# Redealing the opening of a hybrid decoder layer: one load moved to ScalarE's queue, waits by bank, weight splits in another order, forget gates later and their series on VectorE

## The chip, the cores and the metric

The kernel runs on one core of a Trainium2 chip. The metric is the device time of one execution in microseconds. The kernel before was run three times; the profile is a fourth execution, taken by the hardware profiler. All times within it count from its first instruction.

## The reference, cut to what matters

One decoder layer over x of 512 x 2048, in float32:

```python
h = rms_norm(x, g_pre)
proj = einsum('bsd,de->bse', h, w_in)          # q, k, v, gate of three head groups, and six forget logits
out_a = moba_attention(...)                    # 6 heads, causal, T5 bias
log_f = log_sigmoid(fb + b_forget)
out_b = forgetting_attention(..., log_f)       # 6 heads, bias by the running sum of log_f
mkv = einsum('bmd,de->bme', rms_norm(mem, g_mem), w_mem_kv)
out_m = memory_attention(...)                  # 4 heads into 256 memory tokens
y = concatenate([out * silu(gate) for each group])
o = einsum('bse,ed->bsd', y, w_out)
x = x + rms_norm(o, g_post)
```

## The kernel before, in words

**Numbers.** Every large product runs at float32 precision as three passes: an operand is split into a high half (ScalarE copies it to the rounded type) and a low half (VectorE subtracts the high half), and `three` multiplies high x high, low x high, high x low. So each weight piece of 128 x 1024 goes: DMA into `raw`, ScalarE to `ring` half 0 (L985, `hi`), VectorE to `ring` half 1 (L1394, `minus`), TensorE. `ring` has three slots, so the high half of piece n waits until piece n-3 is used; `raw` has six.

**Stages.** First the memory part: 256 memory tokens are turned by TensorE (`turn_tiles(0, ...)`), taken from PSUM by ScalarE (`hi_memory`) and VectorE (`lo_memory`) in eight banks, and multiplied with w_mem_kv in eight strips of two pieces each (`strip`; `hi_mem`, `lo_mem`). Strips 0 to 3 give K, 4 to 7 give V; VectorE scales each by the token norms (`k_mem`, `copy_v_mem`), which TensorE spreads over the partitions by `spread_rstd` in strip 1. During strips 1 to 5 the x tiles are squared, scaled, turned in strips 3 to 6 and taken as tokens (`take_tokens`, L1053 to L1061 and L1479). The bias table of the T5 heads is made by TensorE in strip 3 and copied by VectorE (L1629) in strip 5.

Then 28 projection pairs of 128 columns each. Both dimensions are halved, and each pair takes seven products (TOK_A to TOK_G) of 128 x 1024 weights by 1024 x 256 tokens instead of eight; some operands are sums of weight quarters (VectorE, L1421, `add_weights`) or of token quarters. Four token operands are "late" (TOK_B, C, E, G): `hi_late` and `lo_late` split them after the last strip, in `LATE_ORDER`. The attention of the head before is dealt over the products of a pair (`attention`, `after_operand`). Pairs 0 to 3 are queries and gates of the memory heads; pair 4 on are the other heads.

The forget logits are six columns; `forget_gates` multiplies them as a narrow stationary operand `wf` with four token operands, TOK_E last, before pair 0. ScalarE and VectorE sum the two halves in `fbuf` (L1222, L1668), POOL makes -|z| (L1884, L1885, which raises f_neg), ScalarE takes Exp in pair 0 (L1236), VectorE a reciprocal at the end of pair 1 (L1690), and POOL the series of the logarithm (L1890 to L1898) on 6 x 512 values. VectorE scans the sum at the end of pair 3 (L1693).

Last the output projection, in the same way, in 52 steps of one piece each (`STEPS`; five ring slots). Each step is 12 matmuls of 128 x 512. `y_work(n)` deals the making of its token operands over the steps: VectorE makes TOK_B at n = 6, TOK_C's sum at 8, TOK_B's low half at 9.

**What sets the order.** Everything is written out by hand: each engine runs its own list in order and waits on semaphores. SyncE issues all loads of weights in the order of use; whatever it waits for holds up all loads behind it. It loads g_post (L603, L604) between steps 10 and 11, once `y_raw` has told that the last head is gated, because g_post lies where its gate buffer was. ScalarE issues only two loads at the very start (L1170).

What the steps of the change touch: in the tensor block L645 (`strip`), L814, L821, L849, L850; in the scalar block L1065, L1174 to L1222, L1234, L1346; in the vector block L1456, L1596 to L1669, L1688; in the gpsimd block L1889 to L1898; in the sync block L603, L604.

## Time and profile before

| | us |
|---|---|
| median of 3 runs | 918.08 |
| lowest, highest | 917.96, 918.86 |
| the profiled execution, its own time | 920.29 |
| its span, first to last instruction | 918.5 |
| busy TensorE (PE), VectorE (DVE), ScalarE (ACT), GpSimd (POOL) | 884.9, 694.8, 503.6, 106.1 |
| mean granted TensorE clock | 0.985 |

Matmuls are pipelined, so a busy TensorE says only that it has work; gaps and the granted clock say where it has lost time. A granted clock of 1.00 is 2.4 GHz, 0.50 is 1.2 GHz. In a row of the timeline the first number is the start, the second the length of the merged stretch, and the brackets give the idle time before it and what ended it.

### The profile page before, as it was taken

How to read it: one execution, taken by the hardware profiler on the slowest of the kernel's cores; microseconds unless marked ns; L12 is line 12 of the kernel's file. 1: busy time of each engine (PE TensorE's matmuls, PEld its weight loads, DVE VectorE, ACT ScalarE, POOL GpSimd, SP SyncE). 2: the span in 40 equal slices, each digit the busy share in tenths (PEclk: the TensorE clock that was granted, in tenths of full speed). 3: DMA queues.
4: the chain of work that ended last, by engine and by line, in shares of the span. 5: the costliest groups of instructions: out<-in, count | busy, mean ns of one | idle time of the engine just before them, and what ended most of it. 6: DMA issues, size and time to landing. Idle time of an engine off the chain costs nothing.

```text
span 918.5 us, 16262 instructions
## 1 busy us (share of the span) xinstructions
PE 884.9 (96%) x6525; PEld 841.8 (92%) x6525; DVE 694.8 (76%) x965; ACT 503.6 (55%) x882; POOL 106.1 (12%) x103
## 2 busy tenths in 40 slices
PE   8997998999999999999999999999999999799995
PEld 5887998999999999999999999999999988688884
DVE  4889978987777777777777778787877784975558
ACT  5795554555646464646464646464646474555552
POOL 0000406811111001010021212020202000000000
PEclk9999999999999999999999999999999999899998
DMA  9955476469979566975567774444444496466755
GB/s 299 294 135 151 145 246 194 112 128 201 195 145 197 129 195 133 265 151 142 167 155 160 230 166 111 104 103 105 104 104 104 159 359 225 151 209 198 282 198 184
DMA packets 178641, 161.54 MB, mean 176 GB/s; under 512 B 6969, under 2 KB 143833, under 8 KB 177286
## 3 DMA queue, kind: packets, MB, share of 16 engines
q1 hardware_dynamic: 169574, 142.67, 51.6%
q0 software_dynamic: 8704, 16.78, 12.5%
q8 instruction: 52, 0.85, 0.4%
q10 hardware_dynamic: 288, 1.05, 0.3%
q14 instruction: 23, 0.19, 0.1%
HBM read 152.33 MB, written 43.28 MB: 213 GB/s over the span
## 4 chain that ended last, share of the span: by engine, by line
PE 79%; DVE 13%; ACT 5%; issue 3%; DVEq 0%; POOL 0%; ACTq 0%; POOLq 0%
PE d_ps L630 12%; PE d_ps L632 12%; PE d_ps L631 12%; PE e_ps L630 6%; PE e_ps L632 6%; PE e_ps L631 6%; PE c_ps L630 3%; PE c_ps L632 3%; PE c_ps L631 3%; DVE ring L1394 3%; PE pt_ps L777 3%; PE score_ps L631 1%; PE score_ps L630 1%; PE score_ps L632 1%; DVE sums L1421 1%
## 5 line engine op out<-in xcount | busy, mean ns | idle before, releaser
L1394 DVE TENSOR_TENSOR ring<-raw,ring 128x1024 fp32r<-128x1024 f32 x134 | 165.2, 1237 | 67.9 <-ACT ring L985 67.4
L1394 DVE TENSOR_TENSOR ring<-sums,ring 128x1024 fp32r<-128x1024 f32 x112 | 140.2, 1253 | 96.1 <-ACT ring L985 95.7
L630 PE MATMUL d_ps<-tok_hi,ring 128*128 128x256 f32 x672 | 191.7, 285 | 2.9 <-DVE ring L1394 2.9
L632 PE MATMUL d_ps<-tok_lo,ring 128*128 128x256 f32 x672 | 190.8, 284 | 0.0
L631 PE MATMUL d_ps<-tok_hi,ring 128*128 128x256 f32 x672 | 190.7, 284 | 0.0
L985 ACT ACTIVATE ring<-raw 128x1024 fp32r<-128x1024 f32 x134 | 141.3, 1059 | 72.9 <-PE d_ps L632 46.8
L630 PEld LDWEIGHTS d_ps<-tok_hi,ring 128*128 128x128 f32 x672 | 129.5, 193 | 3.3 <-issue 3.3
L632 PEld LDWEIGHTS d_ps<-tok_lo,ring 128*128 128x128 f32 x672 | 129.6, 193 | 0.0
L631 PEld LDWEIGHTS d_ps<-tok_hi,ring 128*128 128x128 f32 x672 | 129.5, 193 | 0.0
L985 ACT ACTIVATE ring<-sums 128x1024 fp32r<-128x1024 f32 x112 | 117.9, 1053 | 19.8 <-DVE sums L1421 18.1
L1421 DVE TENSOR_TENSOR sums<-raw 128x1024 f32<-128x1024 f32 x56 | 70.2, 1253 | 0.6 <-issue 0.3
L1421 DVE TENSOR_TENSOR sums<-sums,raw 128x1024 f32<-128x1024 f32 x56 | 70.3, 1255 | 0.0
L630 PE MATMUL c_ps<-tok,ring 128*128 128x256 f32 x224 | 64.4, 287 | 0.0
L630 PE MATMUL e_ps<-tok_hi,ring 128*128 128x256 f32 x224 | 64.3, 287 | 0.0
L630 PE MATMUL e_ps<-tok,ring 128*128 128x256 f32 x224 | 64.3, 287 | 0.0
L632 PE MATMUL e_ps<-tok_lo,ring 128*128 128x256 f32 x224 | 63.4, 283 | 0.0
L631 PE MATMUL d_ps<-tok,ring 128*128 128x256 f32 x224 | 63.4, 283 | 0.0
L632 PE MATMUL d_ps<-tok,ring 128*128 128x256 f32 x224 | 63.4, 283 | 0.0
L632 PE MATMUL c_ps<-tok,ring 128*128 128x256 f32 x224 | 63.4, 283 | 0.0
L630 PE MATMUL d_ps<-tok,ring 128*128 128x256 f32 x224 | 63.4, 283 | 0.0
L631 PE MATMUL e_ps<-tok_hi,ring 128*128 128x256 f32 x224 | 63.4, 283 | 0.0
L631 PE MATMUL c_ps<-tok,ring 128*128 128x256 f32 x224 | 63.4, 283 | 0.0
(375 smaller groups left out, 2204.7 us busy)
## 6 DMA issues: line engine op xcount, KB each, us to landing
raw<-in_w_in_dram SPq DMA_DIRECT2D x112, 512.0 KB, 6.2
sum_dram<-in_w_out_dram POOLq DMA_DIRECT2D x32, 512.0 KB, 7.4
raw<-sum_dram SPq DMA_DIRECT2D x32, 512.0 KB, 3.8
raw<-in_w_out_dram SPq DMA_DIRECT2D x24, 512.0 KB, 6.4
raw<-in_w_mem_kv_dram SPq DMA_DIRECT2D x16, 512.0 KB, 8.3
sum_dram<-in_w_out_dram SPq DMA_DIRECT2D x4, 2048.0 KB, 11.9
stage<-in_x_dram SPq DMA_DIRECT2D x4, 1024.0 KB, 9.5
xres<-in_x_dram SPq DMA_DIRECT2D x4, 1024.0 KB, 7.3
```

What stands on the lines that cost most here:

```text
L630: pe.matmul(dst, lhs[0], rhs[0], start=start, stop=False, skip_group_check=True)
L631: pe.matmul(dst, lhs[1], rhs[0], start=False, stop=False, skip_group_check=True)
L632: return pe.matmul(dst, lhs[0], rhs[1], start=False, stop=stop, skip_group_check=True)
L777: last = pe.matmul(bank[:, first:S], v, pT[:, hl_p, kb, first:S] if not head.memory else pT_mem[:, hl_p, kb, first:S], start=(hl_v, hl_p, ...
L985: act.activation(dst, src, ACTF.Copy).then_inc(hi_done, 1)
L1394: return dve.tensor_tensor(dst, a_, hi_.bitcast(F32), ALU.subtract)
L1421: dve.tensor_tensor(sum_tile(p, s), one, two, ALU.add).then_inc(sum_done, 1)
```

## The change

The load of g_post leaves SyncE's list. ScalarE issues it in step 5 of the output projection, after its own wait for the same semaphore:

```diff
@@ sync
             load_steps(9, 11)
-            sp.wait_ge(y_raw, NH)
-            sp.dma_start(gpost[:], g_post.partition_broadcast(P)[:, 0, :]).then_inc(gpost_landed, 16)
             load_steps(11, X_AFTER[0])
@@ scalar, y_work
                 if n == 5:
                     act.wait_ge(y_raw, NH)
+                    act.dma_start(gpost[:], g_post.partition_broadcast(P)[:, 0, :]).then_inc(gpost_landed, 16)
                     hi_y(TOK_D, LAST_TILE, LAST_TILE + 1)
```

TensorE's two waits for four and eight banks of memory tokens become one wait per bank inside strip 0. The splits of weights and tokens are dealt in another order on ScalarE and VectorE: weight pieces go between the banks and ahead of other work of a strip, and the table copies go from VectorE to ScalarE.

```diff
@@ tensor
+                        if t == 0 and k % 2 == 0:
+                            pe.wait_ge(bank_taken, kt // 2 + 1)
                         last = three(d_ps[t % 2][:, 0:NMEM], (w[:, 0, k], w[:, 1, k]), (memT[:, 0, kt], memT[:, 1, kt]),
...
-                if t == 0:
-                    pe.wait_ge(bank_taken, 8)
...
-            pe.wait_ge(bank_taken, 4)
@@ scalar
             hi_memory(2, 4)
-            hi_memory(4, 6)
             hi_mem(1)
-            hi_memory(6, 8)
+            hi_memory(4, 8)
             for t in range(STRIPS_MEM):
...
-                hi_next(0)
+                if t != 1:
+                    hi_next(0)
+                hi_next(1)
                 if 1 <= t <= NM:
...
-                hi_next(1)
+                if t == NM + 1:
+                    for i, (bank, lo_, hi_) in enumerate(table_banks):
+                        act.wait_ge(table_made, i + 1)
+                        act.activation(table[:, lo_:hi_], bank[0:NA, 0:hi_ - lo_], ACTF.Copy).then_inc(table_copied, 1)
                 if t == 0:
...
                     root(1, 0, MB)
+                    hi_mem(4)
@@ vector
-            lo_memory(0)
+            lo_memory(0, 2)
             lo_mem(0)
+            lo_memory(2, 4)
             lo_mem(1)
-            lo_memory(1)
+            lo_memory(4, 8)
...
+            def lo_next(t, half):
+                if t + 1 < STRIPS_MEM:
+                    lo_mem(2 * (t + 1) + half)
+                else:
+                    add_weights(0, half + 1)
+                    lo_operand(0, half)
             for t in range(STRIPS_MEM):
+                if t > 0:
+                    lo_next(t, 0)
                 if t == 1:
...
+                if t > NM:
+                    copy_v_mem(t - 1)
+                if t == 0:
+                    lo_next(t, 0)
+                lo_next(t, 1)
                 if 1 <= t <= NM:
...
-                if t > NM:
-                    copy_v_mem(t - 1)
-                for half in range(2):
-                    if t + 1 < STRIPS_MEM:
-                        lo_mem(2 * (t + 1) + half)
-                    else:
-                        add_weights(0, half + 1)
-                        lo_operand(0, half)
-                if t == NM + 1:
-                    for i, (bank, lo_, hi_) in enumerate(table_banks):
-                        dve.wait_ge(table_made, i + 1)
-                        dve.tensor_copy(table[:, lo_:hi_], bank[0:NA, 0:hi_ - lo_]).then_inc(table_copied, 1)
```

The late operands come in the order B, C, E, G. The splits of E and G, and the gate products with TOK_E, move into pair 0, and so does what follows from them. `wf` lies at the place of `pT` and is cleared by POOL after 16 turned banks instead of by VectorE in strip 4.

```diff
-LATE_ORDER = [TOK_E, TOK_B, TOK_C, TOK_G]
+LATE_ORDER = [TOK_B, TOK_C, TOK_E, TOK_G]
@@ tensor
-            pe.wait_ge(late_ready, 1)
-            forget_gates(2, TOK_E, slice(T2, S), final=True).then_inc(f_done, 1)
...
                     product(p, i)
+                    if p == 0 and i == TOK_D:
+                        pe.wait_ge(late_ready, LATE_ORDER.index(TOK_E) + 1)
+                        forget_gates(2, TOK_E, slice(T2, S), final=True).then_inc(f_done, 1)
                     attention(p, i)
@@ scalar, after the strips
-            hi_late(TOK_E)
+            hi_late(TOK_B)
             hi_v_mem(2)
             hi_operand(0, 2)
-            hi_late(TOK_B)
             hi_v_mem(3)
             hi_late(TOK_C)
-            hi_late(TOK_G)
-            act.wait_ge(f_done, 1)
-            act.activation(fbuf[:, 1], f_ps[32:32 + NB, :], ACTF.Copy).then_inc(f_low, 1)
@@ scalar, after_operand
-                if p == 0 and i == TOK_D:
+                if p == 0 and i == TOK_A:
+                    hi_late(TOK_E)
+                if p == 0 and i == TOK_B:
+                    hi_late(TOK_G)
+                if p == 0 and i == TOK_E:
+                    act.wait_ge(f_done, 1)
+                    act.activation(fbuf[:, 1], f_ps[32:32 + NB, :], ACTF.Copy).then_inc(f_low, 1)
+                if p == 0 and i == TOK_G:
                     act.wait_ge(f_neg, 1)
                     act.activation(fbuf[:, 1], fbuf[:, 2], ACTF.Exp).then_inc(f_exp, 1)
@@ vector, after the strips
-            dve.tensor_tensor(token_f32(TOK_G), token_f32(TOK_G), token_f32(TOK_C), ALU.subtract).then_inc(late_f32, 1)
-            lo_late(TOK_E)
+            lo_late(TOK_B)
             lo_v_mem(2)
             lo_operand(0, 2)
-            lo_late(TOK_B)
+            dve.tensor_tensor(token_f32(TOK_G), token_f32(TOK_G), token_f32(TOK_C), ALU.subtract).then_inc(late_f32, 1)
             lo_v_mem(3)
             lo_late(TOK_C)
-            lo_late(TOK_G)
-            dve.wait_ge(f_low, 1)
-            dve.scalar_tensor_tensor(out=fbuf[:, 0], in0=f_ps[0:NB, :], scalar=bfor[:, 0:1], in1=fbuf[:, 1],
-                                     op0=ALU.add, op1=ALU.add).then_inc(f_z, 1)
@@ vector, after_operand
+                if p == 0 and i == TOK_B:
+                    lo_late(TOK_E)
+                if p == 0 and i == TOK_C:
+                    lo_late(TOK_G)
+                if p == 0 and i == TOK_E:
+                    dve.wait_ge(f_low, 1)
+                    dve.scalar_tensor_tensor(out=fbuf[:, 0], in0=f_ps[0:NB, :], scalar=bfor[:, 0:1], in1=fbuf[:, 1],
+                                             op0=ALU.add, op1=ALU.add).then_inc(f_z, 1)
@@ gpsimd
+            pool.wait_ge(bank_turned, 16)
+            pool.memset(wf[:].bitcast(F32), 0.0).then_inc(wf_cleared, 1)
```

The series leaves POOL, where it was 21 instructions, for VectorE, where multiply and add go together: 12 instructions, one after each product of pair 2 and the first five of pair 3, each waiting for the one before.

```diff
@@ vector
+            def forget_series(n):
+                z, e, s2, p = fbuf[:, 0], fbuf[:, 1], fbuf[:, 2], fbuf[:, 3]
+                last = len(SERIES) + 3
+                if n > last:
+                    return
+                dve.wait_ge(f_series, n + 1)
+                if n == 0:
+                    dve.tensor_tensor(e, e, p, ALU.mult).then_inc(f_series, 1)
+                elif n == 1:
+                    dve.tensor_tensor(s2, e, e, ALU.mult).then_inc(f_series, 1)
+                elif n == 2:
+                    dve.tensor_scalar(p, s2, SERIES[0], None, ALU.mult).then_inc(f_series, 1)
+                elif n < last - 1:
+                    dve.scalar_tensor_tensor(out=p, in0=p, scalar=SERIES[n - 2], in1=s2, op0=ALU.add, op1=ALU.mult
+                                             ).then_inc(f_series, 1)
...
+                if 2 <= p < NM:
+                    forget_series(PRODUCTS * (p - 2) + i)
@@ gpsimd
-            pool.wait_ge(f_rec, 1)
-            chain(pool.tensor_tensor(e, e, p, ALU.mult))
...
-            pool.tensor_tensor(z, p, z, ALU.subtract).then_inc(f_parts, 1)
```

## Rows read from the trace of the kernel before

**Rows 1.** The page, section 2: slices of the span, TensorE's granted clock.

```profile
PEclk9999999999999999999999999999999999899998
```

**Rows 2.** Waits of TensorE over the whole span: who for whom, us, times, longest.

```profile
PE c_ps L630 <- issue: 5.5, 1, 5.5
```

**Rows 3.** Windows by stage: opening, pairs 1 to 4, the restart at 786.73.

```profile
13.97:96.20 82.23, 69.50 (x528) 66.08 (x528) 74.78 (x144) 60.01 (x107) 0.00 (x0) 0.94 0.70 200
...
116.36:140.21 23.85, 23.85 (x196) 23.59 (x195) 17.70 (x26) 14.42 (x29) 0.00 (x0) 1.00 0.72 226
140.21:169.08 28.87, 26.04 (x196) 25.27 (x194) 25.33 (x28) 13.37 (x29) 22.76 (x14) 0.94 0.53 156
169.08:194.24 25.16, 24.35 (x196) 23.68 (x194) 21.57 (x27) 13.89 (x29) 12.49 (x9) 1.00 0.66 137
194.24:218.28 24.04, 24.04 (x196) 23.66 (x194) 19.76 (x29) 14.34 (x31) 2.96 (x4) 1.00 0.82 176
...
786.73:791.98 5.25, 5.25 (x12) 4.14 (x13) 5.25 (x5) 2.03 (x3) 0.00 (x0) 0.50 0.44 154
```

**Rows 4.** Timeline of SyncE before the output projection's step 11.

```profile
748.26 3.58 SPq L507 DMA_DIRECT2D raw<-in_w_out_dram  x2
765.59 0.34 SPq L604 DMA_DIRECT2D gpost<-in_g_post_dram  x1
```

**Rows 5.** Timeline of ScalarE in the output projection, steps 5 to 7.

```profile
764.97 1.06 ACT L985 ACTIVATE ring<-raw 128x1024 fp32r<-128x1024 f32 x1 [1.66 <-PE score_ps L632]
...
772.42 1.06 ACT L985 ACTIVATE ring<-raw 128x1024 fp32r<-128x1024 f32 x1 [6.08 <-DMA raw<-in_w_out_dram]
...
775.29 0.58 ACT L1307 ACTIVATE waste_o<-score_ps 128x512 bf16<-128x512 f32 x1
...
776.97 1.92 ACT L1276 ACTIVATE tok_hi<-tok_f 128x2048 fp32r<-128x2048 f32 x1 [0.23 <-DVE tok_f L1741]
```

**Rows 6.** Timeline of VectorE there: TOK_B's low half.

```profile
784.35 2.28 DVE L1394 TENSOR_TENSOR tok_lo<-tok_f,tok_hi 128x2048 fp32r<-128x2048 f32 x1
```

**Rows 7.** Timeline of TensorE around the hole.

```profile
780.80 0.39 PE L632 MATMUL pt_ps<-ring,tok 128*128 128x512 f32 x1
786.73 0.77 PE L630 MATMUL c_ps<-ring,tok_hi 128*128 128x512 f32 x1 [5.54 <-issue]
```

**Rows 8.** Timeline of TensorE in the opening: two of its gaps.

```profile
16.85 0.36 PE L630 MATMUL d_ps<-memT,ring 128*128 128x256 f32 x1 [2.88 <-DVE ring L1394]
...
82.88 0.44 PE L707 MATMUL c_ps<-ident,vT 128*128 128x128 f32 x2 [2.37 <-DVE vT L1547]
```

**Rows 9.** Timeline of VectorE in the opening.

```profile
15.49 1.21 DVE L1394 TENSOR_TENSOR ring<-raw,ring 128x1024 fp32r<-128x1024 f32 x1
...
23.78 2.29 DVE L1635 CUSTOM_DVE_ANT_0 waste_mem<-stage 128x2048 bf16<-128x2048 f32 x1
...
62.03 1.07 DVE L1646 MEMSET wf<- 128x1216 f32 x1 [0.20 <-issue]
...
65.68 0.67 DVE L1629 COPY table<-c_ps 6x512 f32<-6x512 f32 x1
...
82.42 0.40 DVE L1547 TENSOR_TENSOR vT<-d_ps,rstd_mem 128x256 f32<-128x256 f32 x1
```

**Rows 10.** Timeline of POOL: its first work on the forget gates.

```profile
101.58 6.24 POOL L1884 TENSOR_SCALAR fbuf<-fbuf 6x512 f32<-6x512 f32 x1 [99.06 <-DVE fbuf L1668]
...
109.19 1.49 POOL L1886 TENSOR_SCALAR fbuf<-fbuf 6x512 f32<-6x512 f32 x1
```

**Rows 11.** Timeline of ScalarE in pair 0: the table load ahead of Exp.

```profile
109.27 1.28 ACT L1236 ACT_TABLE_LOAD   x1
```

**Rows 12.** Timeline of VectorE: logits' sum, reciprocal, a sum of weights in pair 2.

```profile
100.76 0.73 DVE L1668 SCALAR_TENSOR_TENSOR fbuf<-pt_ps,bfor,fbuf 6x512 f32<-6x512 f32 x1
...
141.80 3.33 DVE L1690 RECIPROCAL fbuf<-fbuf 6x512 f32<-6x512 f32 x1
...
151.85 2.29 DVE L1421 TENSOR_TENSOR sums<-sums,raw 128x1024 f32<-128x1024 f32 x1
```

More of the change, by code:

```diff
@@ L249, in build @@
         ones, _ = place("ones", [P, P], F32, at=bias_low_at + 4 * 2 * NMEM)
-        wf, _ = place("wf", [P, 4, KH, 38], F32R, at=vT_at + 4 * NMEM)
+        wf, _ = place("wf", [P, 4, KH, 38], F32R, at=pT_at)
         hot, _ = place("hot", [BUCKETS + 1, TABLE], F32, at=tok_at + 4 * 2 * 2 * KH * T2)
@@ L354, in build @@
         f_den = sem("f_den")
-        f_rec = sem("f_rec")
+        f_series = sem("f_series")
         f_pool = sem("f_pool")
@@ L1064, in hi_late @@
             def hi_late(i):
-                if i == LATE_ORDER[0]:
+                if i == TOK_B:
                     act.wait_ge(used, MEM_PIECES)
@@ L1454, in scale_tile, with lo_memory @@
                 dve.tensor_scalar(one, one, stat[:, 4, t:t + 1], None, ALU.mult).then_inc(tile_scaled, 1)
-            def lo_memory(half):
-                for b in range(4 * half, 4 * half + 4):
+            def lo_memory(b0, b1):
+                for b in range(b0, b1):
                     dve.wait_ge(bank_hi, b + 1)
@@ L1645, in _ @@
                 if t == 4:
-                    dve.memset(wf[:].bitcast(F32), 0.0).then_inc(wf_cleared, 1)
                     dve.wait_ge(forget_landed, 32)
@@ L1658, in _ @@
             dve.wait_ge(bank_taken, TURNS)
-            dve.tensor_tensor(token_f32(TOK_G), token_f32(TOK_G), token_f32(TOK_C), ALU.subtract).then_inc(late_f32, 1)
-            lo_late(TOK_E)
+            lo_late(TOK_B)
             lo_v_mem(2)
             lo_operand(0, 2)
-            lo_late(TOK_B)
+            dve.tensor_tensor(token_f32(TOK_G), token_f32(TOK_G), token_f32(TOK_C), ALU.subtract).then_inc(late_f32, 1)
             lo_v_mem(3)
             lo_late(TOK_C)
-            lo_late(TOK_G)
-            dve.wait_ge(f_low, 1)
-            dve.scalar_tensor_tensor(out=fbuf[:, 0], in0=f_ps[0:NB, :], scalar=bfor[:, 0:1], in1=fbuf[:, 1],
-                                     op0=ALU.add, op1=ALU.add).then_inc(f_z, 1)
+            def forget_series(n):
[13 more added lines that the diff above has]
+                                             ).then_inc(f_series, 1)
+                elif n == last - 1:
+                    dve.scalar_tensor_tensor(out=p, in0=p, scalar=1.0, in1=e, op0=ALU.add, op1=ALU.mult
+                                             ).then_inc(f_series, 1)
+                else:
+                    dve.wait_ge(f_pool, 4)
+                    dve.tensor_tensor(z, p, z, ALU.subtract).then_inc(f_parts, 1)
             def before_operand(p, i):
@@ L1687, in after_operand @@
                     second_strip(p, i)
+                if p == 0 and i == TOK_B:
[6 more added lines that the diff above has]
+                                             op0=ALU.add, op1=ALU.add).then_inc(f_z, 1)
                 if p == 1 and i == TOK_G:
                     dve.wait_ge(f_den, 1)
-                    dve.reciprocal(fbuf[:, 3], fbuf[:, 3]).then_inc(f_rec, 1)
+                    dve.reciprocal(fbuf[:, 3], fbuf[:, 3]).then_inc(f_series, 1)
+                if 2 <= p < NM:
+                    forget_series(PRODUCTS * (p - 2) + i)
                 if p == NM - 1 and i == TOK_G:
@@ L1888, in _ @@
             pool.tensor_scalar(p, e, 2.0, None, ALU.add).then_inc(f_den, 1)
-            pool.wait_ge(f_rec, 1)
-            chain(pool.tensor_tensor(e, e, p, ALU.mult))
-            chain(pool.tensor_tensor(s2, e, e, ALU.mult))
-            chain(pool.tensor_scalar(p, s2, SERIES[0], None, ALU.mult))
-            for c in SERIES[1:]:
-                chain(pool.tensor_scalar(p, p, c, None, ALU.add))
-                chain(pool.tensor_tensor(p, p, s2, ALU.mult))
-            chain(pool.tensor_scalar(p, p, 1.0, None, ALU.add))
-            chain(pool.tensor_tensor(p, p, e, ALU.mult))
-            pool.tensor_tensor(z, p, z, ALU.subtract).then_inc(f_parts, 1)
             def add_term(g, i):
```

## Prediction, made before the changed kernel was built or run

> **What bounds the kernel now.** I read the page first: TensorE's granted clock is full except in the first four slices of ten or so and in one late slice [rows 1]. The waits of TensorE name the largest single hole, 5.5 us with releaser "issue" [rows 2]; the others are shorter ones behind VectorE, nearly all in the opening, two of them in [rows 8]. The windows by stage show how uneven the run is [rows 3]: from 13.97 to 96.20 us, before the first projection product, TensorE is busy 69.50 of 82.23 us at a mean clock of 0.94 while VectorE is busy 74.78; pairs 1 and 4 of the projection take 23.85 and 24.04 us with no idle TensorE; pairs 2 and 3 take 28.87 and 25.16. So three places hold time: the opening, pairs 2 and 3, and one hole near 781 us. Elsewhere TensorE is full, and nothing the change touches lies there.
>
> **The hole at 781 us.** SyncE issued its last weight loads at 748.26 and then waited for the last head's gated output; g_post went out at 765.59 and the next weight piece only after it [rows 4]. That piece, for output step 11, is what ScalarE waited 6.08 us for, until 772.42 [rows 5]. Everything then ran late in a row: ScalarE's split of TOK_B at 776.97 [rows 5], VectorE's low half at 784.35 for 2.28 us [rows 6], TensorE idle from 781.19 to 786.73, 5.54 us [rows 7]. The restart was paid too: 12 matmuls in 5.25 us at clock 0.50 [rows 3], so about 2.6 us lost.
> With g_post on ScalarE's queue the load of step 11 goes at about 753, so step 11 is split when its ring slot is free. ScalarE split step 10 at 764.97 [rows 5]; a step is half of those 5.25 us and a little, 2.7 us, so step 11 comes at 767.7 instead of 772.42. Then, by the written order: VectorE low half of 11 to 769.9, TOK_B's difference 2.2 to 772.1; ScalarE splits step 12 at 770.4, two squares (0.8 each, the first row of them in [rows 5]) to 772.8, TOK_B to 774.7, step 13 to 775.7; VectorE step 13 to 776.9, TOK_C's sum to 779.1, step 14 to 780.3, TOK_B's low half to 782.5. TensorE starts at 782.7, not 786.73: 4.0 us sooner, after 1.5 us of idle. What is late next is thus VectorE's own order, not a load. In the opening the idle of 2.88 us [rows 8] was followed by half clock, another of 2.37 was not [rows 8]; for a shorter one I take it that the clock stays and add 2.5. **+6.5 us**, 4.0 to 6.5. The added DMA issue on ScalarE stands ahead of the split of TOK_D's last tile. SyncE's row for it is 0.34 us [rows 4]; the step behind it began 0.8 us after that tile was ready, which covers it. If it took the several us that SyncE's issues sometimes take with full rings, 1 to 3 us would come back.
>
> **The opening.** TensorE's first strip waited 2.88 us [rows 8] for a low half that VectorE did only after four banks of memory tokens, at 15.49 [rows 9]. After two banks it can start at 13.2, so the strip starts at 14.4 and runs with the banks, to 20.9 instead of 24.5. But the next gate is VectorE's: the square sum at 23.78 [rows 9] moves only by the 1.1 us that VectorE saves, and the spread of the norm comes 4.1 us behind it, at 26.8. TensorE, ready at 24.4, now waits 2.4 us there. I take this as even odds for one stretch of half clock, 1.0 us by the time it reaches VectorE. From there ScalarE and VectorE set the pace. ScalarE's first token bank starts at 40.6 instead of 44.7 (VectorE's K tile holds it). The table copies (0.67 us the first of two, 0.94 together) and the memset of wf (1.07) leave VectorE [rows 9]; the copies' 0.85 goes on ScalarE, which is full there. VectorE's last token tile: 4.1 - 0.85 + 1.07 + 0.94 = 5.3 us sooner, so at 77.1, not 82.4 [rows 9]. The memset on POOL stands behind 16 turned banks (48 us) and is wanted at 63: even at the 6.24 of POOL's slowest row [rows 10] it is done by 55.
> Then a new order bites: the V tile that TensorE turns next (at 82.42 until now [rows 9]) comes behind one sum and one low half, so at 79.4. TensorE, done with the strips at 75.0, waits 4.8 us and starts at half clock, 1.5 us on the gate products. These (48 narrow matmuls, two turns, the marker) take 6.3, so pair 0 starts at 87.6, not 96.20 [rows 3]. TOK_E's gate products, 1.8 us, now lie inside pair 0. Late operands: VectorE has TOK_B's low half at 84.9, TOK_C's at 91.2, TOK_E's at 98.0, TOK_G's at 101.7; TensorE wants them at 90.5, 93.4, 99.2 and 106.8. Pair 1 starts at 109.6 instead of 116.36 [rows 3], 6.8 us sooner, or 5.8 with the lower clock at 27. **+6.2 us.** Weight loads take no part: each piece had landed before the time at which its split now stands, the tightest by half a us.
>
> **Exp at the end of pair 0.** The logits' sum (0.73 us [rows 12]) comes behind last_two of TOK_E, at 106.7; then POOL's first instruction, which took 6.24 us against 1.49 for a like one [rows 10], and a difference of 1.3: f_neg at 115. ScalarE arrives for Exp at 110.7 and stands 4.3 us, then loads a table, 1.28 [rows 11], does Exp and two gates before it seeds c_ps: 118.0. Behind it stand VectorE's gate halves and, on TensorE, TOK_C of pair 1, ready at 116.8: 1.2 us, and with VectorE's work pushed back about 0.7 more before pair 1 ends. **-1.9 us.**
> Whether 6.24 comes back is the one price I can't read off. POOL's instruction ran while VectorE had two-input instructions back to back, and these kept their normal length. By the Trainium skill, "SBUF — State Buffer", section "SBUF: two separate sides", a GpSimd instruction that reads SBUF and a VectorE one with two SBUF inputs exclude each other, the first to start keeping the ports for its whole length. By that rule alone the wait is one VectorE instruction, L1884 lasts under 2.7 us, f_neg comes 3.5 us sooner and no wait is left; the row's 6.24 says more, so the sum goes by the row.
>
> **The series in pairs 2 and 3.** While POOL works through it, VectorE's sums last up to 2.29 us [rows 12] where 1.2 is normal; some ten instructions are stretched, 5 to 7 us in all. That goes. In its place VectorE gets 12 instructions over 6x512, one per product. The nearest row is the logits' sum of the same shape and kind, 0.73; the far bound is the reciprocal, 3.33 [rows 12]. I take 0.65 from start to start, 7.8 in all. The two pairs now exceed a clean 24.0 by 4.9 and 1.1. The reciprocal stays and still makes pair 2's TOK_E late, by 1.3 us (0.5, and 0.8 from the delay above). In both pairs the probabilities' low half has two series steps ahead of it: 1.1 us of waiting before P times V, twice. New excess 3.5 against 6.0. **+2.5 us**, 0 to 4.5. POOL's adds into w_out sums start some 60 us sooner, beside DMA queues with room. The scan at the end of pair 3 is not nearer to any need.
>
> **Sum.** 6.5 + 6.2 - 1.9 + 2.5 = 13.3 us. The profiled execution took 920.29 us (span 918.5): 907.0. The median of the runs is 2.2 lower, 918.08: **904.8 us**.
>
> **Rivals.**
> (a) POOL's first instruction is quick: one VectorE instruction of 1.2 us ahead of it and 1.49 of its own, so no wait for Exp, 1.9 us back and 0.8 in pair 2: 902.1. For it: no other POOL row is near 6 us. Against: this one was, and it is still POOL's first of that kind. Chance 0.22. The rule cited above from "SBUF — State Buffer" of the Trainium skill would give this.
> (b) The gaps are kept, in other places: half clock after the 1.5 us gap at 781 (-1.7), after 26.8 (-1), a longer stall for Exp (-1.4): 908.9. For it: of the two gaps in [rows 8] one was followed by half clock, and the hole at 781 was. Chance 0.20.
> (c) The opening gives nothing, since ScalarE, not VectorE, ends last (it is full from 45 to 62 and gets the copies), the rest as forecast: 911. Chance 0.04.
> (d) Slower: the 6x512 steps cost as the reciprocal does, 3.33. 12 x 2.7 = 32 us more on VectorE in two pairs in which it has no slack left; with the forecast's 13.3 the run ends near 937. The point from which it decides: 13.3 over 12, so at 1.8 us a step. Against: the reciprocal is a slower kind of operation than multiply and add. Chance 0.03.
> (e) g_post's move frees nothing since step 12 waits for its sum in DRAM: that had long been added (its load went out at once after step 11's), so 0.01: 911.3.
> The forecast keeps 0.50.
>
> **Numbers.** A measurement of this kernel tells 0.2%, 1.8 us, from no change. Range 900.0 to 910.5: below, (a) with a full clock in the opening and cheap series steps; above, (b) with 1.5 us more from the series. Of the cases only (d) ends off the faster side; 0.02 is left for (b) and (c) together with a cost nobody named: faster 0.95, same 0.02, slower 0.03.
>
> **What would show it.** A wait of TensorE of 1 to 2 us where "issue" had 5.5; SyncE without a pause at 751 to 765; pair 0 at 87 to 89 and a wait of 4 to 5 us just before; POOL's L1884 successor at about 6 us and ScalarE's Exp idle before it; VectorE's sums in pairs 2 and 3 all near 1.2; steps near 0.7. Wrong would be a wait of over 3 us at 781, or pair 4 starting later than 189 us.

## The result, and the profile after

The changed kernel is faster, by less than was forecast. Seven executions of it took 909.57 to 916.03 us, median 914.14, where seven of the kernel before took 915.26 to 921.46, median 918.82. The ratio is 0.994, 95% interval 0.9914 to 0.9966. The forecast was 904.8 us and the top of its range 910.5. The profiled execution took 910.54 us (span 908.7), one of the two shortest of the seven. The seven spread over 6.5 us, those of before over 6.2.

TensorE's clock on the page [rows 1] no longer has the dip at the start of the output projection:

```profile
PEclk9999999999999999999999999999999999999999
```

The waits of TensorE over the whole span of after (who for whom, us in total, times, longest) answer to [rows 2] and [rows 8]:

```profile
PE c_ps L707 <- DVE vT L1554: 4.2, 1, 4.2
PE pt_ps L777 <- DVE pT_mem L1401: 4.0, 3, 2.1
PE c_ps L809 <- DVE rstd_diag L1651: 2.0, 1, 2.0
...
PE c_ps L628 <- issue: 1.3, 1, 1.3
PE d_ps L628 <- DVE ring L1401: 1.1, 2, 0.9
PE d_ps L628 <- ACT out_six L1338: 1.0, 1, 1.0
```

The "issue" wait is 1.3 us where it was 5.5. The 4.2 us for the V tile and the 2.0 us for the spread of the norm are the two that the forecast had in the opening. The last line, a wait for ScalarE's out_six, is new. And "pT_mem", the probabilities' low half, has a 2.1 us wait that no step of the forecast has. The windows by stage, in the order of [rows 3] (the opening, pairs 0 to 5), say where it is:

```profile
14.38:88.78 74.40, 66.46 (x512) 63.01 (x512) 67.70 (x138) 55.99 (x106) 1.11 (x1) 0.95 0.77 219
88.78:110.82 22.04, 22.04 (x187) 21.97 (x185) 21.05 (x20) 12.09 (x15) 2.12 (x1) 1.00 0.67 202
110.82:134.66 23.84, 23.84 (x196) 23.59 (x195) 17.60 (x26) 16.01 (x31) 8.29 (x6) 1.00 0.86 230
134.66:162.06 27.40, 24.98 (x195) 23.73 (x194) 23.86 (x33) 13.56 (x29) 2.68 (x3) 1.00 0.91 208
162.06:187.94 25.88, 24.66 (x195) 23.69 (x194) 22.34 (x34) 13.76 (x29) 2.70 (x3) 1.00 0.80 171
187.94:214.19 26.25, 24.11 (x196) 23.64 (x194) 19.80 (x29) 14.35 (x31) 3.58 (x4) 1.00 0.77 162
```

Pair 0 starts at 88.78 (96.20 before), pair 1 at 110.82 (116.36), so 5.5 us are won there. Pairs 2 and 3 take 53.28 us for 54.03. Pair 4 takes 26.25 for 24.04, and 2.2 us are given back. From pair 5 to the start of the last pair, pair 27, the two traces run in step (502.41 us for 502.47). The rest is won behind it, in the output projection: from there to the end it takes 192.15 us for 197.75.

### The profile page after: what moved, and what is told of

Its sections match the earlier page's. It is cut to its first block, busy times and chain, and to the rows that moved or that the text cites. A ratio compares the mean times of both kernels' runs of the same rounds, so it can differ in the third digit from the quotient of the medians.

```text
span 908.7 us, 16256 instructions
## 1 busy us (share of the span) xinstructions
PE 880.6 (97%) x6525; PEld 837.0 (92%) x6525; DVE 690.4 (76%) x974; ACT 503.0 (55%) x884; POOL 72.0 (8%) x84
## 4 chain that ended last, share of the span: by engine, by line
PE 74%; DVE 14%; ACT 5%; issue 4%; DMA 2%; POOL 1%; SPq 0%; DVEq 0%; ACTq 0%; POOLq 0%
PE d_ps L628 11%; PE d_ps L630 11%; PE d_ps L629 11%; PE e_ps L628 6%; PE e_ps L630 5%; PE e_ps L629 5%; PE c_ps L628 3%; PE c_ps L630 3%; PE c_ps L629 3%; DVE ring L1401 3%; PE pt_ps L777 3%; DMA raw<-in_w_in_dram 2%; DVE sums L1428 2%; PE score_ps L629 1%; PE score_ps L628 1%
## 5 line engine op out<-in xcount | busy, mean ns | idle before, releaser
L1401 DVE TENSOR_TENSOR ring<-sums,ring 128x1024 fp32r<-128x1024 f32 x112 | 137.9, 1231 | 94.8 <-ACT ring L983 94.1
```

The costliest lines, as they stand in the source:

```text
L1401: return dve.tensor_tensor(dst, a_, hi_.bitcast(F32), ALU.subtract)
```

## The experiments

Every run below was timed in turn with the kernel before on its own chip; before's median stood at 918.5 to 919.8 in all four sets. "Series" is the forget gates' series, "adds" are POOL's 32 accumulating DMAs into the sums of w_out in DRAM (L1933).

| run | edit | median (lowest to highest), us | ratio to before, 95% |
|---|---|---|---|
| e1 | before, g_post on ScalarE's queue | 913.52 (911.55 to 915.22) | 0.9937 (0.992 to 0.9954) |
| e2 | after, g_post back on SP's | 913.21 (911.43 to 913.80) | 0.9933 (0.9918 to 0.9949) |
| e3 | after, adds held to pair 5 | 908.17 (906.70 to 909.79) | 0.9881 (0.9864 to 0.9898) |
| e4 | after, series back on POOL | 910.30 (908.94 to 910.88) | 0.9904 (0.9889 to 0.9919) |
| e5 | after, unchanged | 909.92 (908.36 to 912.63) | 0.9909 (0.9891 to 0.9926) |
| e6 | e3 and e2 | 913.17 (912.22 to 913.96) | 0.9943 (0.9931 to 0.9956) |
| e7 | e4 and e2: the opening and the late gates alone | 915.71 (913.00 to 917.52) | 0.9966 (0.9952 to 0.9979) |
| e8 | e3, V tile's copy first | 906.87 (905.96 to 907.02) | 0.987 (0.9857 to 0.9883) |
| e9 | before, unchanged | 918.98 (916.97 to 921.55) | 0.9994 (0.9982 to 1.0006) |
| e10 | after, unchanged | 911.76 (909.09 to 916.21) | 0.9919 (0.9897 to 0.994) |
| e11 | e3, eight steps of the series left out | 905.80 (905.20 to 906.80) | 0.9854 (0.984 to 0.9868) |
| e12 | e8, reciprocal and series in VectorE's gaps | 901.48 (900.55 to 902.05) | 0.981 (0.9797 to 0.9824) |

### g_post alone, and taken back (e1, e2, e6)

```diff
 e1, on the kernel before
-            sp.wait_ge(y_raw, NH)
-            sp.dma_start(gpost[:], ...).then_inc(gpost_landed, 16)
...
                     act.wait_ge(y_raw, NH)
+                    act.dma_start(gpost[:], ...).then_inc(gpost_landed, 16)
```

> The kernel before with one part of the change alone: g_post is loaded from ScalarE's queue (in y_work, n == 5) and not from SP's. Theory of the prediction: the hole of 5.54 us ahead of the PE restart at 786.73 is gone or about 1.3 us as in the trace of after, no clock of .50 follows it, and the whole is 4.0 to 6.5 us shorter than before (ratio 0.993 to 0.996, some 912.8 where before is 918.8). Rival 1 (half the gain is only in the profile: the stretch of half clock does not follow the hole in every execution of before): the profile shows -5.8 and the timed runs -3 to -4 us. Rival 2 (g_post frees nothing): within 0.2% of before.

e1 gained 5.0 us. Its TensorE waits show the hole at 1.3, and the new wait behind it:

```profile
PE c_ps L628 <- issue: 1.3, 1, 1.3
...
PE d_ps L628 <- ACT out_six L1330: 0.9, 1, 0.9
```

The stretch that follows, 782.91 to 793.90 in e1, ran at clock 1.00. So the mechanism is as forecast, with 0.95 us, which the forecast had not, handed back 23 us later: ScalarE reaches the copy of product C (out_six) after a split of TOK_F's operand, and TensorE now comes there first.

> The kernel after with g_post back on SP's queue (after load_steps(9, 11), behind the wait for y_raw), all else as changed. Prediction: the hole and the half clock at the output's start come back, 5.8 us over the profile of after, and the timed runs stand 4 to 6.5 us over after's 914.1: 918 to 920.6. That would leave nothing or +1 us of a gain for the opening, the late gates and the series together, where the profile of after says -4.1 us at pair 5. Rival (the load's place is worth little in most executions and what the rest gives is lost elsewhere): 914 to 916.

e2 missed its expectation of 918 to 920.6 by 5 us. It stood at 913.2, which against the first 914.14 of after looks like no gain at all from a part that e1 shows to be worth 5 us; against e5's 909.92 it is 3.3 us. The hole was back (5.6 us, "issue") with the half clock behind it, but a stall of TensorE in pair 4, which the next section is about, was only 0.14 us in e2's profile where after's has 2.14. e6 asks again, with that stall out of the way:

> The kernel after with POOL's adds held to pair 5 (as in e3) and g_post back on SP's queue (as in e2). With the adds out of the way, e2's question is asked again: e2 came out at 913.2, no slower than after. If g_post's place is worth what e1 shows (5 us), this one stands at 913 to 914 where e3 is at 908.2, and e2's nought is a matter of what else varies in after. If the place is worth nothing once the opening is redealt, it stands at 908 to 909.5.

e6 is 5.0 us above e3, which differs from it in g_post alone (the two ran on different chips; by the distance to before on each it is 4.8). The profiles say the same without help from medians: from the start of pair 27 to the end it takes 192.1 to 192.5 us in all nine with the load on ScalarE's queue, and 197.0 to 197.9 in all five with it on SyncE's, e2 among them. So the place of g_post is worth some 5 us with the old opening and with the new one, and what hid it in e2 lies elsewhere in the kernel.

### What pair 4 lost: the adds (e3, e5, e10)

```diff
 e3, on the kernel after, POOL's program
+            pool.wait_ge(used, operand(5, TOK_A) + 1)
             for u in ADDED_EARLY:
                 add_term(*u)
```

> The kernel after with one wait more on POOL: its adds into w_out's sums begin only at the first product of pair 5 (some 214 us) and not at 117 us. Theory (the adds beside the 2 MB copies and the weight loads make weights land late in pairs 1 to 4, more in some executions than in the one profiled): the 2.14 us stall of TensorE in pair 4 is gone or under 0.5 us, pairs 1 to 4 take at most 102.2 us against 103.4 of after's profile, and the timed runs fall by 2 to 4 us to 910 to 912, with a spread of under 3 us. Rival 1 (the spread comes from the opening: V tile waits, two stretches of half clock): the pair 4 stall goes but the timed runs keep 909.5 to 916, median over 913. Rival 2 (the stall of pair 4 is from SP's own order, negc's store, bias and four weights at once): it stays at about 2 us.

One wait more, and the kernel is at 908.17: faster than any of the three medians of after (914.14, 909.92, 911.76) and than its own expectation, with a spread of 3.1 us. Pair 4 in e3, then pair 4 in e10, the third profile of the unchanged kernel after (window; us long, PE, PEld, DVE, ACT, POOL busy, clock, DMA share, GB/s):

```profile
187.85:211.69 23.84, 23.84 (x195) 23.58 (x194) 19.87 (x29) 14.54 (x31) 0.00 (x0) 1.00 0.41 112
```

```profile
189.27:219.54 30.27, 25.34 (x195) 24.55 (x194) 21.02 (x31) 14.91 (x31) 3.58 (x4) 0.95 0.74 148
```

Two profiles of after beyond the first were taken to see where its slower executions lose:

> The kernel after, unchanged, beside the next three on the same chip. It should come out between 910.5 (its one profile) and 914.1 (its median), and its second profile is what it is run for: theory of the adds: where the execution is slower than the first profile's 910.54, the microseconds are found between pair 1 and pair 5 (weights landed late, stalls ahead of PV products or of VectorE's sums), and the stretches before pair 1 and from pair 5 to the end agree with the first profile within 0.5 us. Rival: they are found in the opening (stretches of half clock at other places).

> The kernel after, unchanged, for a third profile and for a second count of its runs beside before on one chip. By the theory of the adds it stands between 908.4 and 916.0 in single runs, median 910 to 914, with the stall of TensorE in pair 4 anywhere from 0.1 us to 3.4 us, the more the later the third load of that burst landed after pair 4's start (20.7 us for 2.14, 21.9 for 3.35, 18.7 for 0.14), and all pairs outside of pair 4 as in the first profile within 0.3 us.

In pair 4 both went as the theory of the adds has it. The stall ahead of P times V (the probabilities times V) was 2.14 us in the execution of 910.54, 3.35 in that of 912.32 and 4.93 in that of 916.21, the last beyond the 3.4 expected. After the longer two TensorE's clock was half for 3.4 us (from 212.8 in e5, from 216.6 in e10). The opening did not repeat as expected: pair 1 starts 1.1 us sooner than in the first profile in e5, which has no half clock at 27, and 1.3 us later in e10, where half clock stood from 80.1 to 86.9. So the executions differ in both places. The chain, VectorE's row in the first profile of after and then VectorE's and TensorE's in e10:

```profile
208.74 1.23 DVE L1428 TENSOR_TENSOR sums<-raw 128x1024 f32<-128x1024 f32 x1 [2.48 <-issue]
```

```profile
212.87 1.23 DVE L1428 TENSOR_TENSOR sums<-raw 128x1024 f32<-128x1024 f32 x1 [5.28 <-issue]
```

```profile
216.81 1.65 PE L777 MATMUL pt_ps<-pT_mem,kmv 128*128 128x512 f32 x3 [4.93 <-DVE pT_mem L1401]
```

VectorE's next sum of weights stands in its queue ahead of pT_mem and found its weight piece not landed ("issue": nothing on an engine released it; it began within 0.1 us of the landing of the third of the four weight loads that SyncE issues in a row in pair 4, its burst). SyncE's rows and the loads' times, e10 first, then e3:

```profile
193.63 0.36 SPq L555 DMA_DIRECT2D negc_dram<-fbuf  x1
198.91 0.34 SPq L537 DMA_DIRECT2D bias<-toep_dram  x1
199.29 7.94 SPq L507 DMA_DIRECT2D raw<-in_w_in_dram  x4
...
sum_dram<-in_w_out_dram POOLq DMA_DIRECT2D x4, 512.0 KB, 7.5
raw<-in_w_in_dram SPq DMA_DIRECT2D x4, 512.0 KB, 12.0
```

```profile
192.22 0.33 SPq L555 DMA_DIRECT2D negc_dram<-fbuf  x1
194.00 0.34 SPq L537 DMA_DIRECT2D bias<-toep_dram  x1
194.38 4.55 SPq L507 DMA_DIRECT2D raw<-in_w_in_dram  x4
...
raw<-in_w_in_dram SPq DMA_DIRECT2D x4, 512.0 KB, 6.5
```

With four adds in the window a weight piece takes 12.0 us to land in e10 (median of the four; 9.8 to 11.6 in the other eight profiles with adds there), without them 6.5 to 6.8. The adds delay it twice: the small transfers ahead of the burst in SyncE's order come through later, and each piece shares the DMA engines. The first part is seen in the rows: the load of `bias` waits until the store of `negc_dram` has landed, which takes 5.3 us in e10 and 1.8 in e3, so the burst was issued 10.0 us after pair 4's start in e10, against 6.5 in e3, 7.4 in the first profile of after and 8.0 in e5. The Trainium skill, "DMA: Bandwidth & Descriptors", section "Issuing engines are not separate DMA queues", says that DMAs started by the scalar, sync or gpsimd engine run on the same 16 DMA engines and interleave; these rows agree.

The kernel before had four adds in pair 4 too and had no stall there, but it had hardly any slack either. Its row for the same sum:

```profile
212.84 1.23 DVE L1421 TENSOR_TENSOR sums<-raw 128x1024 f32<-128x1024 f32 x1 [0.28 <-issue]
```

VectorE already waited 0.28 us for the piece. Counted from pair 4's start, it wants the piece at 18.3 us, and TensorE's stall is the time by which the sum begins after 18.67, in all eight profiles that have a stall:

| | sum begins, us into pair 4 | TensorE's stall, us |
|---|---|---|
| before; e1; e9 (adds from about 174 to 180 us of the run) | 18.60; 18.85; 18.92 | 0; 0.17; 0.27 |
| e7; e4 (the same, with the new opening) | 19.34; 20.05 | 0.67; 1.39 |
| e2; after; e5; e10 (adds from about 117 us) | 18.81; 20.80; 22.02; 23.60 | 0.14; 2.14; 3.35; 4.93 |
| e3, e6, e8, e11, e12 (adds held) | no wait for the piece | 0 |

That the adds make the stall is shown: with them held it was absent in all five profiles. Not shown is how much of it is their earlier start. Four adds stand in pair 4 in every profile with adds, the stalls of the late and the early ones overlap, and why the piece lands sooner in one execution than in the next stays open beyond the issue time above. Nor do the adds always cost time: e2, with adds, has a median of 913.21 (5.3 us under before on its chip) and e6, the same kernel with the adds held, 913.17 (5.5 under).

### The series (e4, e11)

```diff
 e4, on the kernel after: VectorE loses forget_series, POOL gets its chain back
-                if 2 <= p < NM:
-                    forget_series(PRODUCTS * (p - 2) + i)
...
+            pool.wait_ge(f_series, 1)
+            chain(pool.tensor_tensor(e, e, p, ALU.mult))
+            ...
+            pool.tensor_tensor(z, p, z, ALU.subtract).then_inc(f_parts, 1)
```

> The kernel after with the series of the forget gates back on POOL (all else as changed; POOL's adds come behind it again, at about 175 us and later). Prediction's step: VectorE's steps beside POOL's series cost more, so pairs 2 and 3 have the excess of 6 us of before against 5.3 of after's profile: +0.7, with VectorE's adds of weights at 1.6 to 2.3 us and not 1.21 us. Theory of the adds: the copies of pairs 1 to 3 have no adds beside them, so what the series costs is given back by weights that land in time: the timed runs come out at 912 to 915, no slower than after. Rival (the series' place was worth the 2.5 us that the prediction gave it, and the adds nothing): 915.5 to 917.5.

e4 came out below its expectation of 912 to 915. It is faster than two of after's three medians although it undoes a part that helps. The adds come behind the series there, which is the likely reason, but no run isolates it. Against e3, where the adds are out of the way, it is 2.1 us slower: 1.65 of it in pair 4 and 1.0 in pairs 2 and 3 (54.29 for 53.26 us). VectorE's groups in pairs 2 and 3 of e4, then of e3 (mean ns behind the comma):

```profile
L1428 DVE TENSOR_TENSOR sums<-raw 128x1024 f32<-128x1024 f32 x4 | 6.6, 1644 | 0.0
L1428 DVE TENSOR_TENSOR sums<-sums,raw 128x1024 f32<-128x1024 f32 x4 | 5.9, 1482 | 0.0
```

```profile
L1428 DVE TENSOR_TENSOR sums<-sums,raw 128x1024 f32<-128x1024 f32 x4 | 4.9, 1215 | 0.0
L1428 DVE TENSOR_TENSOR sums<-raw 128x1024 f32<-128x1024 f32 x4 | 4.8, 1210 | 0.0
L1689 DVE SCALAR_TENSOR_TENSOR fbuf<-fbuf 6x512 f32<-6x512 f32 x7 | 4.7, 671 | 0.0
```

The stretching of VectorE beside POOL is gone, as forecast, and the steps cost 0.67 us each. What they cost TensorE is told by e11, which leaves out eight of the twelve steps:

```diff
 e11, on e3: only steps 0, 1, 2 and the last are left
-                last = len(SERIES) + 3
+                last = 3
```

> The kernel after with POOL's adds held to pair 5 (as in e3) and eight of the twelve steps of the forget gates' series left out on VectorE (steps 3 to 10, 6x512 scalar_tensor_tensor of 0.67 us), so the gates are not computed as the reference has them. In e3, pair 2 has stalls of 0.87, 0.30, 0.21 and 0.94 us and pair 3 of 0.20 and 0.93. Theory of the prediction (each step costs VectorE 0.60 to 0.65 us start to start and some of it reaches TensorE): the stalls of 0.94 and 0.93 shrink to about 0 to 0.4, pair 2 takes 26.6 and pair 3 25.1, the whole 1.3 to 1.7 us under e3's 908.2: 906.5 to 907. Rival (the stalls come from the reciprocal and from the weights' sums, the steps lie in VectorE's slack): under 0.4 us of gain.

It gained 2.4 us on e3 (2.6 in the profiles), more than expected: pair 3 fell from 25.87 to 23.83 and pair 2 from 27.39 to 26.79. Its waits in pairs 2 to 4:

```profile
PE d_ps L628 <- DVE ring L1401: 0.9, 1, 0.9
PE pt_ps L777 <- DVE pT_mem L1401: 0.3, 1, 0.3
PE pt_ps L761 <- ACT prob L1156: 0.3, 1, 0.3
PE d_ps L628 <- DVE last_two L1520: 0.2, 1, 0.2
```

Left are mainly the waits in pair 2, behind the reciprocal. So eight of the steps cost 2.6 us in the two pairs as they were placed, and the reciprocal with the other four the remaining 2.9 over twice 23.84.

### The opening (e7, e9, e8)

> The kernel after with the series back on POOL (as in e4) and g_post back on SP's queue (as in e2): what is left of the change is the opening, the late gates and the reciprocal's late place. If the parts add up: e4's 910.3 and the 5 us of e1, 915.3, which is 3.2 us under before: the opening's 6.3 us at pair 1 less some 1.5 us in pairs 2 to 4. If the opening's gain is whole in the timed runs (the prediction's 6.2 less the wait for the Exp), it is 912 to 913.

e7 (e4's and e2's edits together) is 3.0 us under before and 5.4 above e4, so the parts add up. The gain of the opening with the late gates is thus 3.0 us in the timed runs, where the first pair of profiles shows 5.5 at pair 1. e7's own profile wins 4.9 us at pair 1 (half clock stood for 6.8 us before pair 0, from 79.65) and gives 1.1 back before pair 5: 0.3 in pairs 1 to 3, and 0.8 in pair 4, where the stall is 0.67. Another part is luck, and the second profile of before shows it:

> The kernel before, unchanged, for a second profile of it. The first profile's execution took 920.29 us where the median is 918.1 to 918.8, with stretches of half clock at 17.2, 34.3, 92.3, 157.2 and 785.2. Theory (part of what the sum counted as a gain of the opening is the luck of one execution): the second profile has one or two of the stretches before 160 us less, and is 1 to 2 us shorter up to pair 4. Rival: the stretches are the same in every execution, and the difference of 920.29 to the median lies elsewhere.

```profile
13.81:94.46 80.65, 68.11 (x528) 65.03 (x528) 73.23 (x143) 59.83 (x107) 0.00 (x0) 0.96 0.71 204
...
138.82:167.72 28.90, 24.94 (x195) 23.73 (x194) 25.36 (x28) 13.39 (x29) 22.79 (x14) 1.00 0.52 155
```

In e9 the half clock at 92 and at 157 is absent, and pair 1 starts at 114.97 and not at 116.36. Against it e7's pair 1, at 111.48, is 3.5 us sooner. e1, whose opening is that of before, has both stretches again, so e9 alone would not tell which is the rule. The granted clocks of the timed runs do: of the 49 executions of before in the four sets, six have 0.985, the mean of the profiled one with both stretches, and they took 920.33 to 920.82 us; 35 have 0.989 or more, as e9's profiled one has. The stretch at 157 costs nothing: pair 2 takes 28.90 us at full clock and 28.87 with it [rows 3], since the waits behind it soak it up.

```diff
 e8, on e3, in VectorE's loop over the memory strips
             for t in range(STRIPS_MEM):
+                if t == STRIPS_MEM - 1:
+                    copy_v_mem(t - 1)
                 if t > 0:
                     lo_next(t, 0)
...
-                if t > NM:
+                if NM < t < STRIPS_MEM - 1:
                     copy_v_mem(t - 1)
```

> The kernel after with POOL's adds held to pair 5 (as in e3) and, in VectorE's last turn of the memory strips, the copy of the V tile (0.42 us) ahead of the first sum and split of pair 0's weights (1.13 + 1.13 us) and not behind them. TensorE's wait of 4.21 us at 81.01 ends 2.2 us sooner (V tile's turn at 78.7 to 78.8), and nothing takes its place, since the next operands of VectorE are ready ahead of their products: pair 0 starts at 86.2 to 86.6, or at 84.8 if the half clock of 81.6 to 85.0 (1.7 us) goes too; the whole 904.3 to 906. Rival (VectorE has no slack up to pair 0, so the wait turns up again at the forget gates or at pair 0's first product): pair 0 at 88 or later, 907.5 to 908.5.

The V tile's wait went from 4.2 to 1.9 us and no half clock followed, and pair 0 starts at 86.43, as expected. But the gain at pair 1 is 1.4 us over e3's profile and not 2.2 to 3.8: VectorE is busy without a break from 78.40 to 109.35, and the wait turns up again in small pieces: 1.0 us at the next V tile, 0.2 at the single matmul ahead of pair 0 (the marker), 0.4 in pair 0, which takes 22.92 us for 22.04. The median of 906.87 lies between the expectation and the rival; each was half right.

### The gaps of VectorE (e12)

```diff
 e12, on e8
+SERIES_AT = {(2, TOK_B): (0,), (2, TOK_C): (1, 2, 3, 4), (2, TOK_G): (5,),
+             (3, TOK_B): (6,), (3, TOK_C): (7, 8, 9, 10), (3, TOK_E): (11,)}
...
+                if p == 1 and i == TOK_C:
+                    dve.wait_ge(f_den, 1)
+                    dve.reciprocal(fbuf[:, 3], fbuf[:, 3]).then_inc(f_series, 1)
+                for n in SERIES_AT.get((p, i), ()):
+                    forget_series(n)
```

> The kernel of e8 (POOL's adds held to pair 5, the V tile's copy first) with the forget gates' work of VectorE put where VectorE waits 2.92 us for ScalarE in each pair (behind product C's work): the reciprocal of 3.33 us in pair 1's gap and not at that pair's end, and of the series' twelve steps four in the gap of pair 2 and four in that of pair 3, the other four behind products B and G, and B and E. Theory (pair 2's stalls of 0.87, 0.30 and 0.21 us are the reciprocal's, those of 0.94 and 0.93 the steps', as e11's 0.34 in place of 0.94 says): pairs 1 to 3 take 23.8 to 24.3 us each (73.1 to 77.1 in e8, so some 3 to 3.5 us less), the reciprocal lengthens pair 1 by 0.5 us at the most, and the whole is 903.4 to 904.4 where e8 is 906.9. Rival (the gaps are not free: what stands in them delays ScalarE's next splits or product E's taking): 906 to 907.

901.48 us: 17.2 us under before and 8.4 to 12.7 under after. Pairs 2, 3 and 4 of e12:

```profile
133.51:157.35 23.84, 23.84 (x195) 23.59 (x194) 21.63 (x32) 14.00 (x29) 0.00 (x0) 1.00 0.63 188
157.35:181.19 23.84, 23.84 (x195) 23.58 (x194) 22.03 (x34) 13.04 (x29) 0.00 (x0) 1.00 0.39 100
181.19:205.03 23.84, 23.84 (x195) 23.58 (x194) 19.95 (x29) 14.61 (x31) 0.00 (x0) 1.00 0.40 112
```

TensorE has no idle time left in them, with the same work on VectorE: 5.6 us less than e8's pairs 2 and 3, where the expectation had 3 to 3.5, since it summed waits and not times. The reciprocal stands where VectorE waited 2.93 us for ScalarE in each of pairs 1 to 4:

```profile
123.38 3.32 DVE L1767 RECIPROCAL fbuf<-fbuf 6x512 f32<-6x512 f32 x1
126.63 1.15 DVE L1403 TENSOR_TENSOR ring<-raw,ring 128x1024 fp32r<-128x1024 f32 x1
```

## Why the prediction was wrong

The side was right (0.95 on faster) and the likeliest time 9.3 us too low. Of the forecast gain of 13.3 us the changed kernel showed 4.7 (918.82 to 914.14). With the adds held, e3 showed 10.3 (918.50 to 908.17), and 908.17 lies inside the range. So 3.0 us of the shortfall are the sizes of the terms of the sum (the items below come to 4.3, since e7, from which the opening is read, has a stall in pair 4 itself and ran on another chip), and the rest, 5.65 us in the first set, is what the kernel loses beside e3; in e5 and e10 that is 1.55 and 2.26 us. By the prediction's own steps:

- **The step that failed: "POOL's adds into w_out sums start some 60 us sooner, beside DMA queues with room", costed at nothing.** The queues had no room where it counted. Whether the third of four weight pieces lands within 18.3 us of pair 4's start decides there, and the kernel before already missed that by 0.28 us. With the adds pair 4 took 26.25, 28.69 and 30.27 us in the three profiles of after, without them 23.84. In the medians, each against before on its chip, the adds cost 1.55 (e5), 2.26 (e10) and up to 5.65 us (the first set), and 0.24 between e2 and e6. No set ran e3 beside the unchanged kernel after, so these go across chips. The early start as such was not isolated.
- **The hole at 781, +6.5.** Mechanism right: idle 1.28 us for the forecast 1.5, TensorE sooner by 4.26 for 4.0, no half clock. The 0.34 us of g_post's issue on ScalarE cost nothing. Measured 5.0 in the timed runs (e1), 5.5 in the profiles. The missing term is the wait of 0.95 us for ScalarE's out_six at 801; by subtraction 1.7 to 2.2 us are left for the clock, where the forecast took 2.5.
- **The opening, +6.2, and Exp, -1.9.** Together 4.3 forecast, 3.0 measured (e7). The places were near (spread at 26.57 for 26.8, V tile's wait 4.2 for 4.8, pair 1 at 110.82 for 109.6). Too large is the baseline: pair 0 and pair 1 of before were read from an execution with a stretch of half clock at 92.3 that most executions lack by their granted clocks, and without which e9's pair 1 starts 1.4 us sooner. The sum took 2.2 us off because that execution was slow, and then counted part of the same 2.2 as won. The opening also shows its loss of clock only in the windows of [rows 3] (0.94): the digits of [rows 1], read as less than full in the first slices, are 9 there, which stands for 90% or more.
- **Exp** cost TensorE nothing (pair 1 took 23.84), so two errors, this and the baseline's, partly cancel, which is luck. POOL's first instruction took 3.97 us, between the 6.24 of the forecast and the 2.7 at most of rival (a). The forecast also had ScalarE load its table behind the wait for POOL; it loaded it at 112.16, ahead of the wait, stood 1.14 us and had seeded c_ps by 116.0, not 118.0.

```profile
108.70 3.97 POOL L1923 TENSOR_SCALAR fbuf<-fbuf 6x512 f32<-6x512 f32 x1 [56.64 <-DVE fbuf L1721]
```

```profile
112.16 1.28 ACT L1242 ACT_TABLE_LOAD   x1
114.58 0.63 ACT L1242 ACTIVATE fbuf<-fbuf 6x512 f32<-6x512 f32 x1 [1.14 <-POOL fbuf L1924]
```

- **The series, +2.5.** Measured 0.75 in the first pair of profiles and 1.0 between e4 and e3. The steps were priced right (0.60 from start to start for 0.65), and TensorE's waits in the two pairs add up to 3.5 us, just the forecast excess. But the pairs are 5.6 us longer than twice 23.84. Each of the six waits costs some 0.35 more than its row says: eight transposes of the probabilities, say, took 1.36 us from first start to last end behind a wait and 1.03 in e12 without one, and the overlap of 0.16 with the matmul ahead is lost. The excess of before had been measured as time and that of after summed from waits.

Rival (b), "the gaps are kept, in other places", has the nearest number, 908.9 for e3's 908.17, and that is luck. Of its three items only the half clock after 26.8 came (27.0, in five of the eleven profiles with the new opening); the hole at 781 was followed by none, and the stall for Exp was shorter, not longer. The half clock at 81.6 was in the forecast itself.

What stays open: why the first set's executions of after had a median 2.4 to 4.2 us above the later two sets', when before's medians there agree within 1.1 us. The stall of pair 4 varies enough for it, but only profiled executions show it. Half clock had a part: the four at 914.14 us and above have granted clocks of 0.989 to 0.992, where e5's six have 0.993 and 0.994. By an estimate from these, 0.002 of 912 us is 1.8 us of full clock. Where these stretches stood no profile shows.

## What to carry to other kernels

When a change frees a queue early, follow what that queue does next to the one transfer with the least slack, and look in the trace of before for a short wait on it, such as the 0.28 us here: that is where the slack is nought. Put small side work into the gaps that an engine has anyway; the same twelve steps and a reciprocal cost 5.6 us at one per product and nothing with most of them in the gap behind product C. And take two profiles of the kernel before, since a stretch of half clock in the only one is counted as something to win; the granted clocks of the timed runs tell how common it is.

## What the runs showed of the hardware

- POOL's first instruction took 6.24 us in all three profiles of the old opening and 3.97 in all eleven of the new one. Both fit one reading: it ran in the first break between VectorE's instructions with two SBUF inputs. Before, four of these stood back to back until 106.03 and POOL ended at 107.82, that is 1.49 (its normal length) after 106.33; after, two stood there until 110.87 and it ended at 112.67, 1.49 after 111.18. By the Trainium skill, "SBUF — State Buffer", section "SBUF: two separate sides", the first to start keeps the ports for its whole instruction. The rows add that a row of VectorE instructions without a break keeps POOL out from one to the next; that is read from these rows, and no run was made for it alone. After, a VectorE instruction with one of its inputs in PSUM also ended at 111.21, so the place of the break is less sure there.
- A gap is not always followed by half clock: beside the V tile's wait of 4.21 us half clock came in all nine profiles that have this wait, beside the 1.95 us of e8 and e12 in neither. At the spread's wait of 2.05 us it came in the first profile (27.0) and not in e5's and e10's, with the same wait.
- The same program's executions differ by up to 7.1 us (909.09 to 916.21 in e10, with adds in pair 4) and by as little as 1.1 to 1.6 us (e8, e11, e12, with the adds held). The adds alone do not tell the spread: e2 and e4, which have them, spread over 2.4 and 1.9 us, and e3, which has not, over 3.1.
